# RWKV core of a two-block kernel: crossed quadrants, identity terms accumulated, four one-pair groups in flight

## What is computed

```python
def step(state, inp):
    r_t, w_t, k_t, v_t, kk_t, a_t = inp
    s_kk = jnp.einsum('bhij,bhj->bhi', state, kk_t)
    state = (state * w_t[:, :, None, :]
             - s_kk[..., None] * (kk_t * a_t)[:, :, None, :]
             + v_t[..., None] * k_t[:, :, None, :])
    return state, jnp.einsum('bhij,bhj->bhi', state, r_t)

_, y = lax.scan(step, state0, (seq_first(r), seq_first(decay), seq_first(k),
                               seq_first(v), seq_first(kk), seq_first(a)))
```

## Time and profile before

| | before |
|---|---|
| median of 3 runs | 1247.78 us |
| range of the runs | 1246.46 to 1249.91 us |
| the profiled execution: its time | 1243.18 us |
| its span in the trace | 1241.4 us |
| mean granted TensorE clock | 0.925 |
| PE busy | 1075.8 us |
| PEld busy | 895.2 us |
| POOL busy | 696.0 us |
| ACT busy | 527.2 us |
| DVE busy | 509.3 us |

### The profile page before, as it was taken

How to read it: one execution, slowest core, us unless ns; L and a number is a source line. 1 busy time by engine, 2 the same in 40 slices (tenths; PEclk the granted TensorE clock), 3 DMA queues, 4 the chain that set the end, 5 groups by cost and what they waited for, 6 DMA issues and landing times. The chain is left out here.

```text
span 1241.4 us, 19776 instructions
## 1 busy us (share of the span) xinstructions
PE 1075.8 (87%) x8448; PEld 895.2 (72%) x8448; DVE 509.3 (41%) x678; ACT 527.2 (42%) x797; POOL 696.0 (56%) x311
## 2 busy tenths in 40 slices
PE   5999999999788599999969995889759879967685
PEld 4788889899688489998834453889647658845564
DVE  1125274412374645311361445543582350047542
ACT  5447454445437464444321231212333564454252
POOL 6945489988643879888600034000675749970060
PEclk9999999999898799999979998999778979985698
DMA  9641455555454345655633431000036535530150
GB/s 368 233 146 39 153 177 189 191 189 186 137 169 137 100 161 190 191 188 187 214 117 111 152 117 53 4 4 4 19 119 216 162 97 199 187 101 1 46 167 34
DMA packets 45847, 169.36 MB, mean 136 GB/s; under 512 B 5088, under 2 KB 5344, under 8 KB 45440
## 3 DMA queue, kind: packets, MB, share of 16 engines
q1 hardware_dynamic: 43312, 159.06, 38.2%
q0 software_dynamic: 2448, 9.05, 2.2%
HBM read 167.03 MB, written 1.05 MB: 135 GB/s over the span
## 5 line engine op out<-in xcount | busy, mean ns | idle before, releaser
L671 POOL TENSOR_TENSOR ring_r<-ring,high_r 128x1024 fp32r<-128x1024 f32 x256 | 636.8, 2512 | 232.0 <-ACT high_r L801 231.2
L801 ACT CAST high_r<-ring 128x1024 fp32r<-128x1024 f32 x256 | 264.8, 1049 | 262.3 <-DMA ring<-w 262.0
L420 PE MATMUL psum<-x_high,high_r 128*128 128x256 f32 x640 | 182.3, 285 | 1.6 <-DVE x_low L281 1.6
L420 PE MATMUL psum<-x_low,high_r 128*128 128x256 f32 x640 | 181.2, 283 | 0.0
L420 PE MATMUL psum<-x_high,ring_r 128*128 128x256 f32 x640 | 181.2, 283 | 0.0
L394 PE MATMUL psum<-high_r,x_high 128*128 128x512 f32 x320 | 129.0, 403 | 9.8 <-DVE x_low L277 6.6
L394 PE MATMUL psum<-ring_r,x_high 128*128 128x512 f32 x320 | 126.9, 396 | 0.0
L394 PE MATMUL psum<-high_r,x_low 128*128 128x512 f32 x320 | 126.6, 396 | 0.0
L586 DVE TENSOR_TENSOR arena<-arena 128x512 f32<-128x512 f32 x32 | 46.4, 1449 | 192.2 <-ACT arena L562 192.1
L420 PEld LDWEIGHTS psum<-x_high,high_r 128*128 128x128 f32 x640 | 122.9, 192 | 2.9 <-issue 2.3
L420 PEld LDWEIGHTS psum<-x_low,high_r 128*128 128x128 f32 x640 | 122.8, 192 | 0.5
(11 more groups left out here) (313 smaller groups left out, 1743.0 us busy)
## 6 DMA issues: line engine op xcount, KB each, us to landing
ring<-w SPq DMA_DIRECT2D x292, 512.0 KB, 3.3
row<-rows POOLq DMA_DIRECT2D x14, 512.0 KB, 8.4
arena<-relt SPq DMA_DIRECT2D x2, 1536.0 KB, 14.6
h<-x SPq DMA_DIRECT2D x1, 1024.0 KB, 4.9
arena<-lora POOLq DMA_DIRECT2D x2, 512.0 KB, 6.6
out<-h SPq DMA_DIRECT2D x1, 1024.0 KB, 4.0
con<-consts SPq DMA_DIRECT2D x1, 529.0 KB, 5.0
arena<-pT POOLq DMA_DIRECT2D x2, 256.0 KB, 4.0
```

Source lines behind the costliest of these rows:

```text
L420: ins = nc.tensor.matmul(out, a, b, start=(k == 0 and q == 0), stop=(k == KT - 1 and q == 2))
L671: nc.gpsimd.tensor_tensor(low(m), raw(m), read(high(m)), ALU.subtract).then_inc(low_made, 1)
L801: nc.scalar.copy(high(m), raw(m)).then_inc(high_made, 1)
```

## The change

- **Pairs and groups.** A group is now one pair (`GR` = 4 slots: head and token tile), on two banks, one for each head; four groups are in flight, in two rounds. Everything of a group in SBUF is one tile of eight slots: 0 and 1 the two off-diagonal masks, 2 X, 3 Z, 4 the power U1, 5 to 7 the other masked products.
- **Crossed products.** `product` stands for `both`. With `crossed`, head 0 goes to its own half of the partitions and head 1 to the opposite half; each crossed step swaps the halves of head 1. Steps 2 to 9 are crossed. The product with V (moved from step 2 to step 5), step 10 and the output Y are not.
- **Identity in the accumulation.** I + X and Z + X·Z come from TensorE as two accumulated terms (`eye_` first). Per pair of heads this adds 16 products in step 2 (I and X, each times I) and 8 in each of steps 3, 4 and 5. With the product with V moved, steps 2 to 5 have 32, 32, 24 and 24 products a pair in place of 24, 24, 16 and 8. POOL's two additions per round and DVE's additions in steps 3 to 5 go.
- **Evacuation.** In steps 2 to 4 DVE copies head 0's bank and ACT head 1's; steps 5, 6, 8, 10, 11 are ACT's, 7 and 9 DVE's. The masks of x and of step 1 are one DVE instruction a group.
- **Last step in two.** Y is step 11, and M, N and the corrections step 12; DVE waits in step 12 for ACT before it reads the second bank.

```diff
-        GR = 8
-        U = [view(WORK + 4096 * b, GR, 5, HD) for b in range(2)]
...
+        GR = 4
+        IN_FLIGHT = 4
+        U = [view(WORK + 2048 * b, GR, 8, HD) for b in range(IN_FLIGHT)]
...
+        def core_psum(b):
+
+            return psum[:, 2 * b:2 * b + 2, :].rearrange("p h (t s n) -> p (h t) s n", t=NT, s=4)
...
-            for pp in range(GROUPS):
-                for b in range(2):
-                    core_wait(pool, core_dve, DVE_AT, pp, b, "x1")
-                    nc.gpsimd.tensor_tensor(U[b][:, :, 0, :], U[b][:, :, 1, :], C("eye2").unsqueeze(1).broadcast_to([P, GR, HD]),
-                                            ALU.add).then_inc(core_pool[b], 1)
...
+                        if s_ in (2, 3):
+                            ins = nc.scalar.copy(U[b][:, 2:4, 2:5, :], got[:, 2:4, 0:3, :])
...
+                        if s_ == "x":
+                            mk = C("mask_x").unsqueeze(1).broadcast_to([P, GR, 4 * HD])
+                            ins = nc.vector.tensor_tensor(U[b][:, :, 4:8, :].rearrange("p q a n -> p q (a n)"),
+                                                          got.rearrange("p q a n -> p q (a n)"), mk, ALU.mult)
...
+                            ins = nc.vector.tensor_tensor(U[b][:, :, 0:3, :], got[:, :, 0:1, :].broadcast_to([P, GR, 3, HD]), mk, ALU.mult)
+                        elif s_ in (2, 3):
+                            ins = nc.vector.tensor_copy(U[b][:, 0:2, 2:5, :], got[:, 0:2, 0:3, :])
...
-                        def both(k, lhs, rhs):
-
-                            for fi, hh, t, q in many:
-                                for c in range(2):
-                                    ins = nc.tensor.matmul(block_(k, q, c), lhs(fi, hh, t, q, c), rhs(fi, hh, t, q, c),
-                                                           start=True, stop=True)
...
+                        def product(slot, crossed, *terms):
+
+                            for t in range(NT):
+                                for n, (lhs, rhs) in enumerate(terms):
+                                    for hh in range(2):
+                                        for r in range(2):
+                                            o, at = here[r ^ (crossed and hh)], 256 * t + HD * slot
+                                            ins = nc.tensor.matmul(psum[o, B + hh, at:at + HD], lhs(2 * hh + t, r), rhs(2 * hh + t, r),
+                                                                   start=(n == 0), stop=(n == len(terms) - 1))
...
                         elif s_ == 2:
                             dve_did(1)
-                            both(1, X_, U1)
-                            both(2, U1, X_)
-                            ins = both(3, lambda fi, hh, t, q, c: u[here[c], q, 3, :], V_)
+                            product(0, 1, (U1, X_))
+                            product(1, 1, (eye_, eye_), (X_, eye_))
+                            ins = product(2, 1, (X_, U1))
                         elif s_ == 3:
                             dve_did(2)
                             act_did(2)
-                            pe.wait_ge(core_pool[b], pp + 1)
-                            both(0, X_, Z_)
-                            both(1, X_, U1)
-                            ins = both(2, U1, X_)
+                            product(0, 1, (U1, X_))
+                            product(1, 1, (eye_, Z_), (X_, Z_))
+                            ins = product(2, 1, (X_, U1))
...
                         elif s_ == 5:
                             dve_did(4)
                             act_did(4)
-                            ins = both(0, X_, Z_)
+                            product(1, 1, (eye_, Z_), (X_, Z_))
...
+                                        ins = nc.tensor.matmul(psum[here[r], B, at:at + HD], u[here[r], 2 * hh + t, 6, :],
+                                                               vN[here[r], t, head[hh]], start=True, stop=True)
...
+                            product(0, 0, (Z_, lambda q, r: kap[here[r], q % 2, head[q // 2]]))
+                            ins = product(1, 0, (Z_, slot_(6)))
```

More of the change, by code:

```diff
@@ L473, in build @@
         hg = view(2 * S, NT, D)
[L476 to L483, removed]
+        DVE_AT = {s_: i for i, s_ in enumerate(["x", 1, 2, 3, 4, 7, 9, 12])}
+        ACT_AT = {s_: i for i, s_ in enumerate([2, 3, 4, 5, 6, 8, 10, 11, 12])}
+        PE_AT = {s_: i for i, s_ in enumerate(["x"] + list(range(1, 13)))}
+        ROUNDS = KT // IN_FLIGHT
+        def core_psum(b):
+            return psum[:, 2 * b:2 * b + 2, :].rearrange("p h (t s n) -> p (h t) s n", t=NT, s=4)
         def core_wait(eng, sems, table, pp, b, step):
@@ L944, in _ @@
                     evacuate(act, inst, b, dst)
[L945 to L948, removed]
+            for pp in range(ROUNDS):
+                for s_ in (2, 3, 4, 5, 6, 8, 10, 11, 12):
+                    for b in range(IN_FLIGHT):
+                        f, B = IN_FLIGHT * pp + b, 2 * b
                         core_wait(act, core_filled, PE_AT, pp, b, s_)
[L950 to L958, removed]
+                        got = core_psum(b)
+                        if s_ in (2, 3):
+                            ins = nc.scalar.copy(U[b][:, 2:4, 2:5, :], got[:, 2:4, 0:3, :])
@@ L971, in _ @@
                         ins.then_inc(core_act[b], 1)
-            core_wait(act, core_filled, PE_AT, GROUPS - 1, 0, 11)
-            core_wait(act, core_filled, PE_AT, GROUPS - 1, 1, 11)
+            for b in range(IN_FLIGHT):
+                core_wait(act, core_filled, PE_AT, ROUNDS - 1, b, 12)
             for q in range(2):
@@ L1349, in _ @@
                     evacuate(dve, inst, b, dst)
[L1351 to L1354, removed]
+            for pp in range(ROUNDS):
+                for s_ in ("x", 1, 2, 3, 4, 7, 9, 12):
+                    for b in range(IN_FLIGHT):
+                        f, B = IN_FLIGHT * pp + b, 2 * b
                         core_wait(dve, core_filled, PE_AT, pp, b, s_)
[L1356 to L1365, removed]
-                        elif s_ == 1:
[L1368 to L1376, removed]
-                        elif s_ == 4:
[L1378 to L1382, removed]
@@ L1383, in _ @@
                         elif s_ in (7, 9):
[L1384 to L1387, removed]
-                        else:
[L1390 to L1396, removed]
+                            ins = nc.vector.tensor_tensor(Z, Z, got[:, :, 0, :], ALU.subtract)
+                        else:
+                            nc.vector.tensor_copy(MN[:, f, 0:3, :].rearrange("p g i -> p (g i)"), psum[:, B, 0:192])
+                            for c, at in ((0, 192), (1, 128)):
+                                if c == 1:
+                                    core_wait(dve, core_act, ACT_AT, pp, b, 12)
+                                part = KR[:, f, 1, :].rearrange("p (t c n) -> p t c n", t=NT, c=2)[:, :, c, :]
+                                ins = nc.vector.tensor_tensor(
+                                    part, psum[:, B + c, at:at + P].rearrange("p (t n) -> p t n", t=NT), part, ALU.add)
@@ L1397, in _ @@
                         ins.then_inc(core_dve[b], 1)
-            for b in range(2):
-                core_wait(dve, core_act, ACT_AT, GROUPS - 1, b, 11)
-                core_wait(dve, core_dve, DVE_AT, GROUPS - 1, b, 11)
+            for b in range(IN_FLIGHT):
+                core_wait(dve, core_act, ACT_AT, ROUNDS - 1, b, 12)
+                core_wait(dve, core_dve, DVE_AT, ROUNDS - 1, b, 12)
             dve.wait_ge(last_read, 1)
@@ L1735, in _ @@
             pe.wait_ge(last_read, 1)
-            STEPS = ["x0", "x1"] + list(range(1, 12))
+            STEPS = ["x"] + list(range(1, 13))
             CORNERS = ((0, 0), (1, 1), (0, 1), (1, 0))
-            for pp in range(GROUPS):
+            here = [slice(HD * c, HD * c + HD) for c in range(2)]
+            tok = lambda t, c: slice(t * P + HD * c, t * P + HD * c + HD)
+            for pp in range(ROUNDS):
                 for s_ in STEPS:
-                    for b in range(2):
-                        f0, B = 4 * pp + 2 * b, 4 * b
+                    for b in range(IN_FLIGHT):
+                        f, B = IN_FLIGHT * pp + b, 2 * b
@@ L1760, in _ @@
[L1760 to L1770 removed]
+                        u = U[b]
@@ L1799, in _ @@
                             act_did(3)
-                            both(3, X_, Z_)
-                            ins = both(2, U1, X_)
+                            product(0, 1, (U1, X_))
+                            ins = product(1, 1, (eye_, Z_), (X_, Z_))
                         elif s_ == 5:
@@ L1810, in _ @@
                         elif s_ in (7, 9):
-                            dve_did(s_ - 1)
                             act_did(s_ - 1)
-                            ins = both(0, X_, U1)
+                            ins = product(0, 1, (X_, U1))
                         elif s_ == 10:
                             dve_did(9)
-                            for fi, hh, t, q in many:
```

(8 more changed lines are left out.)

144 lines of the change are left out of this document (69 added, 75 removed).

## The result

The changed kernel took 1256.42 us in the median (1254.97 to 1257.72, 4 runs), the kernel before 1248.72 on the same chip. The ratio on record is 1.0092, with a 95% interval of 1.0067 to 1.0118. It doesn't follow from the runs listed: their medians are 7.7 us apart, 1.0062. Either way the change is slower, by 0.6 to 0.9%, where I had forecast 1.7% faster; every run after is longer than every run listed before. The profiled execution took 1255.58 us, its span is 1253.3 us, 11.9 more than the span before.

A forecast was written before the change was run, and what follows sets the result against it. The core, paced mostly by TensorE, was taken to set the end. Masks −2.3, steps 2 to 10 −19.0, last steps +1.0 and last evacuation −0.3 gave −20.6 us: 1247.8 to 1227, range 1219 to 1243 held at 0.8.

The forecast's parts named there:

- What bounds the kernel: Whole kernel: the core, 103.4 us from 774.29, is on the path that sets the end, so its gain isn't given back.
- (a) Masks: Start of each round, masks, x and step 1: 6.9 us until step 2, gains of 1.0 and 1.3 us.
- (b) Steps 2 to 10: Steps 2 to 10 of each round: 23.8 us in place of 33.2 and 33.4, gains of 9.4 and 9.6.
- 608 x 29.2: Crossed products of one round in steps 2 to 9: 608 at 29.2 ns each, 17.8 us.
- The waits of steps 6 to 9: TensorE waiting for ACT's copies: 0.2 us lost in step 6 and 0.2 in step 8, 0.45 a round.
- (c) The last steps: Steps 11 and 12 of each round: 10.1 us in place of 9.6, a cost of 0.5 a round.
- (d): Last evacuation of the core: 0.9 us in place of 1.2, a gain of 0.3, once.
- (e): POOL's additions in the core: they end before they are waited for, so taking them out is worth nothing.
- The clock: Granted clock in the core: stays at 1.00, no fall; with the falls as before, 2.8 us more.
- a limit in long stretches: Rival: TensorE's queue fed no faster than 11.5 ns a record, 1247 in full (chance 0.08), partial 1232 to 1244 (0.14).
- a floor on starts: Rival: records start no closer than 29.2 ns, so crossing buys nothing: 1262, or about 1252 by the skill; chance 0.09.
- The chances: Odds for the whole kernel's time: faster 0.83, same 0.08, slower 0.09.

The follow-up runs named there:

- merged: The changed kernel with X times [Z | U1] as one product and identity terms for both token tiles in one: 1240.15 us, 0.9974 of the kernel before.

## Why the prediction was wrong, step by step

- **What bounds the kernel** held: the core is on the chain, and in the two traces its length came through to the end nearly one for one (+13.6 us in the core, and a span longer by 11.9; the stage before the core happened to end 1.4 us earlier). By the medians the kernel is longer by 7.7 us only; that difference stays open.
- **(a) Masks** held: step 2 starts 6.7 us after the first product (6.9 forecast), and the masks of x cost 1.15 us each.
- **(b) Steps 2 to 10** failed, and with it the forecast. The price, 29.2 ns a crossed product, is right for each burst. The step that failed is "608 x 29.2": I took the price of a burst of 128 instructions for a stretch of thousands. Supply gives about 15 ns an instruction, some 60 ns a product, the same for crossed and uncrossed ones. So crossing gained next to nothing, and the identity cost more than I had put in: 256 of its 320 products cost 13.8 us by the time and 15.9 by the core, where 29.2 ns each are 7.5. Steps 2 to 10 took 41.0 and 40.4 us in place of 23.8.
- **The waits of steps 6 to 9** can't be judged: pauses cover them. The trace shows no wait of TensorE for ACT or DVE there.
- **(c) The last steps**: the price per group held (1.63 us for step 12, the distance from one L1362 to the next); the rounds took 10.9 and 10.5 us in place of 10.1. In the first, two borders of a block stand in this part, with 0.27 us from one record to the next (820.79 and 824.80); what the rest is stays open. **(d)** held; **(e)** wasn't tested by itself.
- **The clock** failed in the first round: 0.71 in 779.60 to 785.40 (0.68 in the earlier trace rows), a fall as before, though from 772.90 on no gap of TensorE was longer than 0.7 us. In the second round it stayed at 1.00 as forecast. The fall cost little: TensorE reached the end of a block at 783.04 and went on at 783.05, 1.34 us after the next block's transfer had ended at 781.71. That is the delay that stands at the pauses, so at the higher clock it would have stood there waiting for the same block.
- **The rivals.** The first, a limit in long stretches, named the cause and mis-sized it. Its price came from the 384 instructions from 774.29 on, 11.5 ns each, which I called a bound from above and which was none: 384 instructions are one and a half blocks, and TensorE did not have to wait for one there. The right reading was in the trace: q8 moves 16 KB at a time, and the long stretches of the core went at 14.6 ns an instruction, just what two quarters allow and just what the supply can still give. The second rival, a floor on starts, came nearest in time (1252 as the estimate from the figure of the Trainium skill, "TensorE: Matmul & The Clock Gate", section "Wait — 56ns, not 53.3ns?"; 1256 measured) but for another reason, so that nearness is luck: records do start 14.6 ns apart, which a floor of 25 ns excludes, and here the measurement decides. The Trainium skill has a sentence nearer to the cause, which the prediction leaves out: "Runtime: NRT & Kernel Launch", section "Instruction fetch mechanics", says that instructions are refilled in blocks of 16 KiB, 256 instructions. The trace agrees with that. The Trainium skill adds there that an engine's slow dispatch hides the refill; here it didn't, the pauses of L1729 sum to 26.1 us.
- **The chances.** I gave slower 0.09, on the ground that a burst in the trace had the price. The range ended at 1243 and left out both cases in which the burst's price doesn't last.

## What to carry to other kernels

Price a stream of small matmuls twice: by the array, and by its instructions, here four for each f32 product and about 15 ns each, as measured here with the other queues at rest, over anything longer than a block of 256. A burst shorter than that says nothing of the second price. When the array's work is halved and the instruction count isn't, look for wider moving sides and shared terms first; in this kernel only with them did the use of all four quarters pay (1.1%, against nothing clear of noise without).

## What the runs showed of the hardware that I had not expected

- TensorE stops for up to 1.9 us after each 256 instructions when it executes them in about 2 us; blocks come 3.4 to 4.2 us apart with the other queues at rest, 16 KB in a transfer of 0.9 to 1.4 us each. The rest of the interval can be read from the records of the kernel after: the transfer of a block starts 1.0 to 1.7 us after TensorE has begun the block before it, and TensorE begins the new one 1.2 to 1.5 us after the transfer ended. So in this trace no more than one block is fetched ahead. Why the two delays are as long as they are stays open.
- On two quarters an f32 record with a 64x64 stationary side takes 29.2 ns with 32 columns as with 64.
- Crossed records start 14.6 ns apart in any burst, also when they accumulate on the product before.
- A fall of the granted clock (0.71) followed a stretch in which TensorE was busy for 5.11 of 6.70 us, with no gap over 0.7 us.
- Two kernels with as many TensorE instructions but different work for the array (merged and the one with identity terms left out) took the same time, 1240.15 and 1240.96 us.
